# A hybrid two-layer block on one core: projecting the un-normalised input, with x loaded in column halves

## What is computed

```python
def rms_norm(x, g):
    y = x * rsqrt(mean(x * x, axis=-1) + EPS)
    return y * g

h = rms_norm(x, g_mix)
z = h @ w_in                       # 1024 x 3072
u, gb, gc, q, k, v = split(z, 6)   # 512 columns each
y_conv = gb * short_conv(gc * u, conv_w)      # causal, width 3
q = rms_norm(q per head of 64, g_q) * 64 ** -0.5
k = rms_norm(k per head of 64, g_k)
y_attn = dilated_mixture(q, k, v)             # 8 heads
mix = concat(rms_norm(y_conv, g_conv_out), rms_norm(y_attn, g_attn_out))
x = x + mix @ w_out
...
```

## Time and profile before

| | us |
|---|---|
| median of 3 runs | 983.71 |
| lowest, highest | 982.75, 985.32 |
| the profiled execution's own time | 984.09 |
| its span in the trace | 982.5 |
| TensorE busy | 965.8 |
| VectorE busy | 679.3 |
| ScalarE busy | 414.1 |
| GpSimd busy | 191.0 |

### The profile page before, as it was taken

The page is one execution under the profiler, slowest core; times in us unless marked ns, Lnnn a source line. Parts: engine busy times, 40 slices in busy tenths (PEclk is TensorE's granted clock), DMA queues, the critical chain, the costliest instruction groups (busy, mean ns, idle before and its releaser), DMA issues.

```text
span 982.5 us, 13933 instructions
## 1 busy us (share of the span) xinstructions
PE 965.8 (98%) x4640; PEld 780.2 (79%) x4640; DVE 679.3 (69%) x1221; ACT 414.1 (42%) x679; POOL 191.0 (19%) x324
## 2 busy tenths in 40 slices
PE   7999999999999999999999999999999999999996
PEld 6777777687888888888888886888888887677886
DVE  6585886697666666755345659389888875785756
ACT  6545454644333333332312126954652225663334
POOL 3010101112000000097300001745680120100000
PEclk9999999999999999999999999999999999999998
DMA  6336756232562333234423222433133463653222
GB/s 214 105 92 199 202 171 183 60 113 86 171 192 85 104 89 106 85 107 130 151 90 102 94 89 86 108 86 87 46 105 86 111 167 86 138 153 127 85 86 108
DMA packets 143190, 115.13 MB, mean 117 GB/s; under 512 B 5452, under 2 KB 131660, under 8 KB 143148
## 3 DMA queue, kind: packets, MB, share of 16 engines
q1 hardware_dynamic: 134748, 85.85, 29.5%
q0 software_dynamic: 8240, 28.73, 10.6%
q10 hardware_dynamic: 160, 0.03, 0.0%
HBM read 100.44 MB, written 4.20 MB: 106 GB/s over the span
## 4 chain that ended last, share of the span: by engine, by line
PE 95%; DVE 3%; ACT 1%; issue 1%; DMA 0%; SPq 0%; DVEq 0%; ACTq 0%
PE bank L653 19%; PE bank L655 19%; PE bank L654 19%; PE bank L919 4%; PE bank L918 4%; PE bank L917 4%; PE bank L636 2%; PE bank L637 2%; PE bank L638 2%; PE bank L687 2%; PE bank L707 2%; PE bank L1134 1%; PE bank L629 1%; PE bank L1133 1%; PE bank L1132 1%; PE bank L843 1%
## 5 line engine op out<-in xcount | busy, mean ns | idle before, releaser
L653 PE MATMUL bank<-hH,wH 128*128 128x512 f32 x808 | 316.7, 392 | 0.8 <-DVE hL L1705 0.5
L655 PE MATMUL bank<-hH,wL 128*128 128x512 f32 x808 | 314.5, 389 | 0.0
L654 PE MATMUL bank<-hL,wH 128*128 128x512 f32 x808 | 314.5, 389 | 0.0
L1638 DVE TENSOR_TENSOR wL<-raw,wH 128x1024 fp32r<-128x1024 f32 x155 | 195.9, 1264 | 156.4 <-ACT wH L1177 156.1
L1177 ACT ACTIVATE wH<-raw 128x1024 fp32r<-128x1024 f32 x155 | 164.0, 1058 | 266.3 <-PE bank L655 120.2
L653 PEld LDWEIGHTS bank<-hH,wH 128*128 128x128 f32 x808 | 151.7, 188 | 39.2 <-issue 7.2
L655 PEld LDWEIGHTS bank<-hH,wL 128*128 128x128 f32 x808 | 151.7, 188 | 31.7
L654 PEld LDWEIGHTS bank<-hL,wH 128*128 128x128 f32 x808 | 151.7, 188 | 31.0
L917 PE MATMUL bank<-aH,wH 128*128 (+1 forms) x160 | 62.2, 389 | 0.0
L918 PE MATMUL bank<-aL,wH 128*128 (+1 forms) x160 | 62.2, 389 | 0.0
L919 PE MATMUL bank<-aH,wL 128*128 (+1 forms) x160 | 62.2, 389 | 0.0
(11 more groups left out here) (466 smaller groups left out, 1543.3 us busy)
## 6 DMA issues: line engine op xcount, KB each, us to landing
raw<-in_w_in_dram SPq DMA_DIRECT2D x61, 512.0 KB, 3.7
mraw<-in_w_mod_dram POOLq DMA_DIRECT2D x24, 512.0 KB, 5.0
raw<-in_w_gate_dram SPq DMA_DIRECT2D x22, 512.0 KB, 3.7
raw<-in_w_up_dram SPq DMA_DIRECT2D x22, 512.0 KB, 3.6
raw<-in_w_down_dram SPq DMA_DIRECT2D x22, 512.0 KB, 3.2
raw<-in_w_out_dram SPq DMA_DIRECT2D x16, 512.0 KB, 3.4
pTd<-turned POOLq DMA_DIRECT2D x24, 320.0 KB, 6.3
x_tok<-in_x_dram SPq DMA_DIRECT2D x4, 512.0 KB, 5.1
```

The costliest lines, as they stand in the source:

```text
L653: mm(o, a, hH[:, k, :], start=(k == 0), stop=False)
L654: mm(o, a, hL[:, k, :], start=False, stop=False)
L655: ins = mm(o, b, hH[:, k, :], start=False, stop=(k == KD - 1))
L1638: TT(wL[s.par][:], raw[s.par][:], wH[s.par][:].bitcast(F32), SU).then_inc(lo_done, 1)
```

## The change

- SyncE loads q's weights first, then x in eight pieces: the first 512 columns of each of the four token blocks, then the second 512. k's weights follow. g_mix gets a DMA and a semaphore of its own, so that its transpose goes first.
- TensorE starts with eight matmuls on a tile of ones. Only one set of transposes is made, of raw x: 22 before the first projection and 10 within it. hH and hL are made from raw x times g_mix, in the banks `HB`; the same banks are copied to xT (`x_copy`; seven by ScalarE, one by VectorE).
- The squares by token follow later. The four columns of 1/rms are spread to a row over all partitions: `diag4` (VectorE) and a matmul with ones (`row_factors`), read as `rb` (ScalarE's copy) and `r2b` (its square). A second, tiny matmul with a permuted identity gives 1/rms in the order in which v's tokens are held.
- Results are scaled: q and k by `rb` and u by `r2b` (`scaled`, VectorE, reading the bank; u, q and k were copied by ScalarE before), v by column when it is copied behind its transposes (four copies of 128 columns, ScalarE, before one of 512). gc's own factor is thus in u's, and gb's is left out: since y_conv is normalised itself, its missing factor is put right in the norm's epsilon, with ssc started at EPS*4/r2b by a reciprocal of 128x512 (VectorE, in `mix(0)`).
- ScalarE's squares of q and k now come behind VectorE's scalings, and `head_sums` waits for them (`sqr_rdy`). `angles()` moves behind a weight split in `mix(0)`, and the silu and the sines with it.

```diff
@@ SyncE
-            for t in range(TB):
-                sp_.dma_start(x_tok[:, t, :], x[0, t * P:(t + 1) * P, :]).then_inc(x_in[t], 16)
...
-            for j, z in enumerate((Z_Q, Z_K)):
-                load(Slot(N_MIX, j), cols(w_in, z))
+            load(Slot(N_MIX), cols(w_in, Z_Q))
+            for h in range(2):
+                for t in range(TB):
+                    c = slice(h * HALF, h * HALF + HALF)
+                    sp_.dma_start(x_tok[:, t, c], x[0, t * P:(t + 1) * P, c]).then_inc(x_in[t][h], 16)
+            load(Slot(N_MIX, 1), cols(w_in, Z_K))
@@ TensorE
+            def x_turn(t, ks):
+
+                pe.wait_ge(x_in[t][ks[0] // KH], 16)
                 for k in ks:
...
+                    ins = transposes(HB[k][:, t * P:(t + 1) * P], [x_tok[:, t, k * P:(k + 1) * P]])
+                    if t == TB - 1:
                         ins.then_inc(xn_mm, 1)
...
+            pe.wait_ge(init_v, 2)
+            for j in range(8):
+                mm(PB[5][:, 0:P], ones[:], ones[:], start=True, stop=True)
...
+            for t in range(TB):
+                x_turn(t, range(KH))
+            x_turn(0, range(KH, KD - 1))
+            x_turn(1, range(KH, KD - 1))
...
-            def head_sums(a, ks):
-
-                freed(pe, ks)
+            def head_sums(a):
+
+                pe.wait_ge(sqr_rdy, a * 2 + 2)
...
+            def project_first():
+
+                pe.wait_ge(lo_done, 1)
+                pe.wait_ge(vec_cp, 1)
+                for k in range(KD):
+                    if k == 2:
+                        x_turn(2, range(KH, KD - 1))
+                        x_turn(3, range(KH, KD - 1))
+                    if k == KH:
+                        pe.wait_ge(xt_a, 1)
+                        for t in range(TB):
+                            x_turn(t, [KD - 1])
+                    pe.wait_ge(h1_done, k + 1)
+                    mm(PB[7][:], blk(wH[0], k), hH[:, k, :], start=(k == 0), stop=False, skip_group_check=True)
...
+            def row_factors():
+
+                pe.wait_ge(dg_rdy, 1)
+                pe.wait_ge(xt_a, 2)
+                mm(PB[3][:], ones[:], diag4[:].rearrange("p b t -> p (b t)"), start=True, stop=True).then_inc(rb_mm, 1)
...
+            project_first()
+            project_second()
+            row_factors()
+            pe.wait_ge(xt_a, 3)
+            project(Slot(2), bank=PB[2])
+            pe.wait_ge(xt_a, KD - 1)
+            mm(PB[6][:, 0:TB], identP[:], sm[:, 4:8], start=True, stop=True).then_inc(pe_pre, 1)
+            pe.wait_ge(rb_rdy, 3)
+            pe.wait_ge(vec_cp, 3)
+            head_sums(0)
@@ ScalarE
+            def qk_squares(first, i, a):
+
+                q, k = (Slot(first, j, 6, i) for j in range(2))
                 wait(act, ss_mm, a * 2)
...
+                split_hi(q.next())
+                freed(act, q)
+                A(sqq[:], qraw[:], ACT.Square).then_inc(sqr_rdy, 1)
+                split_hi(k.next())
+                freed(act, k)
+                A(sqk[HD:P, :], kraw[0:HD, :], ACT.Square)
+                A(sqk[0:HD, :], kraw[HD:P, :], ACT.Square).then_inc(sqr_rdy, 1)
...
-                copy(vtok[:].rearrange("p b n -> p (b n)"), PB[3][:]).then_inc(vt_done, 1)
+                for b in range(TB):
+                    c = (4 if last else 16) + b
+                    ins = copy(vtok[:, b, :], PB[3][:, b * P:(b + 1) * P], sm[:, c:c + 1])
+                ins.then_inc(vt_done, 1)
@@ VectorE
+            def scaled(sl, dst, row, bank=None):
+                used(sl)
+                TT(dst[:], (bank or PB[sl.par])[:], row[:], MU).then_inc(gfree[sl.par], 1)
...
                 u, gc, gb = (Slot(3, j, 6, i) for j in range(3))
+                scaled(u, u_s, r2b)
                 split_lo(u.next())
+                if first:
+                    angles()
+                    need()
+                    mark(v.reciprocal(ssc[:], r2b[:]))
+                    need()
+                    mark(TS(ssc[:], ssc[:], EPS * HALF / P, None, MU))
...
-                normalise(i, None if last else lambda: split_lo(Slot(3, 3, 6, i).next()))
+                def next_query():
+                    scaled(Slot(3, 3, 6, i), qraw, rb)
+                    split_lo(Slot(3, 3, 6, i).next())
+                normalise(i, None if last else next_query)
...
                     conv_low()
                     mod_rows(i, range(0, 2))
+                    scaled(Slot(3, 4, 6, i), kraw, rb)
                     split_lo(Slot(3, 4, 6, i).next())
```

More of the change, by code:

```diff
@@ L766, in _ @@
[L766 to L776 removed]
+            pe.wait_ge(g_in, 16)
@@ new lines, in project_second @@
+            def project_second():
+                pe.wait_ge(hi_done, 2)
+                pe.wait_ge(xt_d, 1)
+                for k in range(KD):
+                    mm(PB[1][:], blk(wH[1], k), hH[:, k, :], start=(k == 0), stop=False)
+                    mm(PB[1][:], blk(wH[1], k), hL[:, k, :], start=False, stop=False)
+                pe.wait_ge(lo_done, 2)
+                for k in range(KD):
+                    ins = mm(PB[1][:], blk(wL[1], k), hH[:, k, :], start=False, stop=(k == KD - 1))
+                ins.then_inc(slot_used, 1)
@@ L1216, in _, with x_copy @@
-            act.wait_ge(init_v, 1)
+            act.wait_ge(init_v, 1)
+            def x_copy(k):
+                act.wait_ge(h1_done, k + 1)
+                copy(xT[:, k, :], HB[k][:]).then_inc(xt_a, 1)
+            act.wait_ge(cst_in, 16)
+            copy(identP[:].rearrange("k (p j) -> k p j", j=TB), ident.rearrange("k (j p) -> k p j", j=TB))
+            split_hi(Slot(0))
+            act.wait_ge(vec_cp, 1)
+            for k in range(KD):
+                act.wait_ge(xn_mm, k + 1)
+                A(hH[:, k, :], HB[k][:], ACT.Identity, scale=vec[:, V_GMIX + k:V_GMIX + k + 1]).then_inc(h1h, 1)
+                if k == KH - 1:
+                    x_copy(0)
@@ L1294, in mix @@
                 used(u)
-                if not first:
-                    wait(act, ych, i + 1)
-                copy(u_s[:], PB[u.par][:]).then_inc(gfree[u.par], 1)
                 split_hi(u.next())
@@ L1659, in _ @@
             v.memset(epst[:], EPS).then_inc(init_v, 1)
-            v.memset(ones[:], 1.0)
+            v.memset(ones[:], 1.0).then_inc(init_v, 1)
             mark(v.memset(cuP[:, 0:2], 0.0))
             def squares(j):
-                dve.wait_ge(x_in[2 * j], 16)
+                for h in range(2):
+                    dve.wait_ge(x_in[2 * j][h], 16)
                 settled(dve)
@@ L1881, in _ @@
             dve.wait_ge(mask_in, 32)
-            for p in range(TB):
-                raw_evac(p)
-            split_lo(Slot(0, 0).next())
+            split_lo(Slot(0, 1).next())
             steps_of_time()
-            angles()
-            split_lo(Slot(0, 1).next())
+            dve.wait_ge(rb_rdy, 2)
             split_lo(Slot(0, 2).next())
```

236 lines of the change are left out of this document (94 added, 142 removed).

## The result

The changed kernel takes 985.13 us (median of 11 runs, 984.62 to 987.02) and the kernel before 983.33 us beside it (11 runs, 982.71 to 985.32): ratio 1.0018, 95% interval 1.001 to 1.0025. A second series of the changed kernel gave 985.36 against 983.58, ratio 1.0015 [1.0006, 1.0024]. The forecast was 983.6, no change. The time lies inside the range, but the move of +1.8 us is real. The difference from the forecast's -0.1 comes from the start, whose gain was smaller than forecast; the rounds as a whole lost a little less than forecast.

A forecast was written before the change was run, and what follows sets the result against it. TensorE, busy 98% of the span, was taken to bound the kernel. The terms -5.7 + 1.7 + 1.1 + 1.4 + 1.4 = -0.1 on 984.09 gave 984.0, as a median 983.6, no change (0.61); range 981.0 to 986.3.

The forecast's parts named there:

- part 1: The start, up to round zero's `mix(0)`: it would begin at 31.4 instead of 37.10, a gain of 5.7 us.
- lower bound of 4.4: Smallest gain allowed at the start, in us, with TensorE's clock up only at 12.9 and halves of x late by 0.4.
- the sign of a mis-sized part 1: At the end of the start: `mix(0)` beginning before 30 or after 33 would show the start's gain mis-sized.
- the landing of x: At the start: the queue carries 390 GB/s, each half follows in 0.67 us, fourth first half at 8.0, last second half at 10.7.
- the clock: At the start: TensorE's clock rises near 10.5, so the first projecting matmul comes at 10.9 instead of 17.30.
- a poor start: Rival, at the start: clock up at 12.9 and halves late add 1.3 us, giving 984.9, no change; chance 0.05.
- the broadcast at 1.2 us: Behind the second projection: the matmul spreading 1/rms takes 0.86 us and two vector transposes 0.35, together 1.2 us.
- the head sums' wait for ScalarE's copies: Ahead of the first head sums: TensorE waits for ScalarE's copies, squares and weight split, 0.6 us late.
- round zero: In `mix(0)`: `angles` (2.5 us) and a reciprocal (4.1 us) on VectorE delay the scores, and TensorE loses 1.7 us.
- the head sums of the next pair: In rounds zero, one and two: TensorE waits for ScalarE's squares behind k's late scaling, 1.1, 1.4 and 1.4 us.
- The scaled k was late: Its rival, in the first three rounds, said the scaled k is not late, 3.9 us less: 979.7, faster; chance 0.15.
- The clock did not fall in the waits: Its rival: the clock falls in pauses ahead of head sums and in first scores, 1.7 us each; two give 987.0; chance 0.13.

The follow-up runs named there:

- c1: Second run of e4's edits (k scaled ahead of `mod_rows`, no reciprocal on VectorE, `angles` early) on the changed kernel: 981.29 us, 0.998 of the kernel before.
- e4: Changed kernel with k scaled ahead of `mod_rows`, the reciprocal replaced by Ln and Exp on ScalarE, and `angles` ahead of u's scaling: 981.46 us, 0.9981 of the kernel before.
- e3: Changed kernel with the reciprocal replaced by Ln and Exp on ScalarE and `angles` moved ahead of u's scaling: 984.36 us, 1.0008 of the kernel before.
- e5: Changed kernel with x loaded in four whole blocks instead of eight halves: 987.58 us, 1.0036 of the kernel before.
- e7: Changed kernel with x's second halves issued only once the second block's first half has landed: 985.82 us, 1.0022 of the kernel before.
- c0: The changed kernel run once more without edits: 985.36 us, 1.0015 of the kernel before.
- e1: Changed kernel with VectorE's scaling of k put ahead of the two rows of `mod_rows`: 981.59 us, 0.9976 of the kernel before.
- e2: Changed kernel with VectorE's reciprocal and its scaling in round zero replaced by Ln and Exp on ScalarE: 984.43 us, 1.001 of the kernel before.
- e9: e4's edits on the changed kernel, with the weight split behind k's scaling also put ahead of `mod_rows`: 981.45 us, 0.9974 of the kernel before.

## Why the prediction was wrong, and where it was right

**The step that failed is part 1's sum, "Gain 5.7".** Over the medians the start gave about 3.4 us: 5.3 lost in the rounds less 1.8 measured, and 3.3 by c1. That is below the forecast's own lower bound of 4.4. And `mix(0)` started at 34.4 in the change's profile, past the 33 that the forecast had named as the sign of a mis-sized part 1. Three terms failed.

The first is the landing of x. The forecast let the queue carry 390 GB/s from the weights on and the halves land in turn, the fourth at 8.0, and by the same 0.67 us the sixth, which the last of the 22 transposes needs, at 9.3. In c1 the sixth was turned from 11.37, in e4 from 11.0, in e3 from 11.8; these three kept the fast pace, so the data alone set it. Two things are behind this: the queue moved 301 to 346 GB/s from 6 to 10 us with halves and 406 with whole blocks (e5), and they shared the queue with those behind them (in e7, without these, the fourth was turned from 8.8, against 9.6 in c0 and 9.8 in c1). How the 2 us divide between the two isn't shown. The first projecting matmul came at 11.3 to 12.95 in the eight profiles with this start, 12.0 in the middle, not 10.9: 1.1 us. The forecast had slow transposes from 6.1 on set this matmul; but where the clock was up early, the data was late. In e1 neither came last, but the low half of h, for which TensorE waited 0.29 us.

The second is the clock, taken to rise at 10.5 from how the kernel before behaved, behind a pause that wasn't there: the warming was forecast to end at 4.5 and lasted until 6.06. By the trace's record it rose between 5.2 and 7.2 in five of the eight (and fell again in two of them), at 10.6 and 11.3 in e2 and e1, and at 14.6 in the change's, behind the forecast's latest case of 12.9. From the first projecting matmul to the first mark pass 19.9 us where the clock is up by then, 20.2 in c0, 20.9 in the change and 21.0 in e9. So a slow clock costs 0.3 to 1.1 us there.

The third is small: the forecast had 19.5 for that stretch, with the clock up, and it took 19.9. In c1 0.1 of the 0.4 us are in the first projection and its ten transposes (6.7 us, forecast 6.6), and 0.3 behind them (13.2, forecast 12.9). One projection had been charged 5.5 us, and the earlier trace rows give 5.74 from 17.30 to 23.04.

The rival "a poor start" (clock at 12.9, halves late by 0.4) named the landing and the clock, at 984.9, 0.2 us under the result, and was given a chance of 0.05. That its number is so close is partly luck. Its start still gave 4.4 us, a full microsecond more than the medians show; its rounds cost 0.3 us more than measured, and its kernel before was 0.4 us slower than the one run beside the change.

By marks the gain is 2.1 to 4.8 us (36.02 less 33.97 and 31.21), 4.0 in the middle, over the 3.4 of the medians. The kernel before has one profile here, and that execution was 0.8 us over the median of the runs beside the change (0.1 to 0.6 over those of the other groups), so its first mark may be late by that much. This stays open.

**Right: the broadcast at 1.2 us**, and the head sums' wait for ScalarE's copies, forecast 0.6 and measured 0.4 beside a tiny matmul.

**Right in mechanism, sizes off: round zero.** The reciprocal was costed at 4.1 us and took 3.34, so 6.5 ns an element against the 7.75 of the slope of the earlier trace rows. The scores waited 1.1 us, not 1.7. The Trainium skill's page VectorE: DVE Perf Modes (First, the fixed hardware budget), by whose repeat count of eight the estimate was 4.3, leads the right way, to a reciprocal far dearer than a plain operation (3.34 against 0.69 for this size), and to a size 29% too high; the measurement decides.

**Right, and the larger part: the head sums of the next pair.** Forecast 1.1, 1.4 and 1.4 us; waits of 0.7, 1.6 and 1.6. e1's rounds show the cause to be the place behind `mod_rows`. The working for rounds one and two had the squares' end 1.4 us behind v's end. In the chain above TensorE has waited 1.3 us when the last square ends at 114.73, and 0.23 more pass until the matmul starts (0.1 in round zero): a step that the sum left out. In round zero the wait was 0.4 us shorter than forecast. It isn't the over-costed reciprocal that makes the difference, since in e2, without any reciprocal on VectorE, the wait is still 0.61; this stays open.

**The rivals.** The scaled k was late, so that one is out. The clock did not fall in the waits of the rounds: the granted clock reads 1.00 there, the matmuls behind them keep the pace of 0.23 us, and the four waits (1.1, 0.7, 1.6 and 1.6 us) make up 4.9 of the rounds' 5.3 us. It did fall at the start, in c0, e5 and e9, a place where the forecast had looked only for a rise. That v's four copies cost nothing in the last round is borne out (40.64 against 40.66).

**The sum as it turned out:** -3.4 + 1.8 + 1.8 + 1.7 = +1.9 us, measured +1.8. This is no test, since the 3.4 come from the medians themselves; with the 4.0 of the marks it would be +1.3. With the forecast's -5.7 in that place the same rounds would have given -0.4.

## What to carry to other kernels

Where a factor is moved from an input to the results, the result's first reader waits for the scaling. Put the scaling in its engine's order right behind the matmul that feeds it, ahead of work that nobody waits for: here that one line was worth 3.9 us in three rounds, of which the last gave 0.4 back, and turned a loss into a gain. An early start should be costed with a rate that was read from pieces of the same row length, for all that is in flight together, and with the clock's rise at its latest place as well as at its likeliest. Distances between marks that every kernel of a series shares, such as the first head sums of each round, tell differences of 0.1 us where medians tell 1 us.

## What the runs showed of the hardware that was not expected

- A reciprocal of 128x512 in full precision took 3.34 us on VectorE; Ln and Exp of the same size took 0.62 and 0.63 us on ScalarE.
- Loads issued together on one queue landed 4.6 to 7.7 us after issue, and 2.8 to 5.2 when the last four were held back (e7); the rate from 3 to 10 us was 238 to 356 GB/s. From 6 to 10 us it was 301 to 346 in ten profiles with pieces of x that have rows of 2 KB, and 406 with rows of 4 KB (e5).
- Eight full-precision 128x128 products took 3.79 us at the slow pace (16 instructions from 2.27), so the warming ends at 6.06, with x, and not 1.6 us ahead of it as the forecast had it.
